# Last input-projection block contracted from the top, attention loads and biases started inside it

## The chip, the cores and the metric

The kernel runs on one core of a Trainium2 chip. The metric is the device time of one execution, in microseconds; lower is better. Engines: PE is TensorE, DVE VectorE, ACT ScalarE, POOL GpSimd, SP SyncE (which here only issues DMAs).

## The reference, cut to what matters

One encoder layer on x of 1024 positions by 2048 channels, float32:

```
h = rmsnorm(x); proj = h @ w_in            # 2048 x 6160: attention q,k,v; mLSTM q,k,v,o; gates
na = neighbourhood attention, 8 heads of 128, 16 x 64 grid, 8 x 16 window, relative bias, softmax
ml = mLSTM forward + backward, 4 heads, q,k through a width-5 convolution and silu first
x += concat(rmsnorm(na), ml) @ w_out
x += expert-choice FFN(rmsnorm(x))         # 16 experts, 128 tokens each, 1024 wide
out = rmsnorm(x)
```

Products are done in three parts: each float32 operand is split in a high and a low part, and high x high, high x low and low x high are summed.

## The kernel before, in words

**Stages.** In order: input projection (12 blocks of 512 output columns), attention, mLSTM, output projection, routing, experts, final norm. TensorE works through them in one fixed order; every engine has its own hand-written instruction order, and semaphores tie them.

**Projection block.** The normed input, transposed, stands in `a_hi` and `a_lo`, each 16 slices (contraction index k) of 4096 bytes a partition. The weights of a block come as 8 chunks of two slices through a ring of four (`raw`, filled by SP; `whi` by ACT, L902; `wlo` by DVE, L1226). Blocks 0 to 5 give `rows` (values, gates of the output), blocks 6 to 11 `feats` (mLSTM q,k; then attention q and k of heads 0 to 3 in blocks 8, 9, of heads 4 to 7 in 10, 11). `feats_block` (L1726 on, products at L1740) goes k = 0 to 15, for each k over four groups of two PSUM banks, 24 products of 128 x 512 per k. After each second k but the last it adds 1 to `w_used`, seven a block; in the last k each bank adds 1 to `bank_ready`. Blocks 6 to 11 run in a hardware loop on TensorE.

**Eviction and store.** DVE (`evict_feats`) multiplies each of 8 banks by the row scale into one of four `stage` slots; POOL (`store`) issues a DMA of it to memory and, when an earlier one has landed, frees its slot (`stage_free`). So banks 4 to 7 wait for landings of banks 0 to 3.

**Memory reuse.** Attention's buffers lie over the projection's. In bytes of a partition: `naq`, `nak`, `nav` (q, k, v of two heads) at 126464 to 159232, which is `a_hi` slices 8 to 15; `prob` from 192000 and `skew` (bias windows) from 200192, which is `a_lo` slices 8 and up; `qrows` at 175616, `a_lo` slices 4 and 5; `nmask`, `bias0`, `bias1` at 27648 to 55296, over the end of `raw`, over `whi` and the start of `wlo`; `na_out` at 60416, over the end of `wlo`, over `stage` and further.

**Start of the attention.** SP waits at L500 and L501 for block 11's `bank_ready`, then issues for heads 0 and 1: 8 windows `skew` (L432), q (L456), k (L457), 16 pieces of v (L466); then `qrows`, `decbc`, `mixg`; then heads 2 to 7, windows after `bias_ready`, q and k after `qk_done`, v after `pv_done` of the head two before. From head 4 on mLSTM loads stand between. POOL, after its stores of block 11, makes `nmask` (L752) and the bias tiles of head h (L757), six each.

**Attention itself.** 64 units, 8 a head. Unit v on TensorE: transpose of `prob` (L1790), score product of unit v + 3 (L1782), value product of unit v - 1 (L1802). DVE adds the bias and takes the maximum (L1382, L1386), ACT takes exp (L1004) and evicts the transpose (L1012), DVE writes the output `na_out` (L1395, `finish`). In unit 1 DVE waits for all stores of the projection, since `na_out` lies over `stage`. Outputs of units 0 and 1 lie over `wlo` only, the third is the first over `stage`.

Of the kernel before, what the change touches and what calls it, by code (L numbers as in the profile page):

```python
# [16 lines left out]
P = 128  # L17
SEQ, D = 1024, 2048
TT = SEQ // P
KD = D // P  # L20
NAH, HD = 8, 128
# [9 lines left out]
BW = 512  # L31
BLK = 12
ROWBLK = 6
OBLK = 4
CPB = KD // 2
RING = 4
GWC = KD * 16 + 32
QR, QC, WR, WC = 8, 16, 12, 32
# [50 lines left out]
def trunk(nc, t):  # L89
    ctx = ExitStack()  # L90
    with ctx:
# [9 lines left out]
        colm = sb("colm", [P, 3, WC])  # L101
        rowm = sb("rowm", [P, 2, WR])
# [13 lines left out]
        stage = sb("stage", [P, 4, BW], F32, proj)  # L116
# [3 lines left out]
        rstd_bc = sb("rstd_bc", [P, 1024], F32, proj)  # L120
        t3 = stage[:, 0:2, :].rearrange("p a b -> p (a b)")
        wide = ExitStack()
        a_hi = sb("a_hi", [P, KD, SEQ], F32R, wide)
# [23 lines left out]
        def place(at, *items):  # L147

            stack = ExitStack()
            if at > ROOM:  # L150
                stack.enter_context(nc.sbuf_tensor("below_" + items[0][0], [P, (at - ROOM) // 4], F32))
            made = [stack.enter_context(nc.sbuf_tensor(name, shape, F32)) for name, shape in items]
            stack.close()
            return made
# [6 lines left out]
        skew, = place(200192, ("skew", [P, 2, 16, 48]))  # L161
        nmask, bias0, bias1 = place(27648, ("nmask", [P, 6, WR, WC]), ("bias0", [P, 6, WR, WC]), ("bias1", [P, 6, WR, WC]))
        biases = (bias0, bias1)
        qrows, = place(175616, ("qrows", [P, 2, SEQ]))

        mv0, mv1, mbc0, kn1, wexp, kw, qkw = place(
            93696, ("mv0", [P, TT, DV + 1]), ("mv1", [P, TT, DV + 1]), ("mbc0", [P, 2, SEQ]), ("kn1", [P, TT, DK]),
# [60 lines left out]
        last = ExitStack()  # L228
        eraw = sb("eraw", [P, 2 * EDEEP, 1024], F32, last)
        last.close()  # L230
        last = ExitStack()
# [7 lines left out]
        ps = ctx.enter_context(nc.psum_tensor("ps", [P, 8, BW], F32))  # L239

        S = {}
# [15 lines left out]
        stsem = [S[f"st{i}"] for i in range(4)]  # L257
# [9 lines left out]
        nqsem, nkvsem, nbsem, mlsem = ([S[n + "0"], S[n + "1"]] for n in ("nq", "nkv", "nb", "ml"))  # L267
# [139 lines left out]
        def _(sp):  # L407
# [51 lines left out]
            def fetch_v(h):  # L459

                hb = h % 2
                for c in range(4):
                    for r in range(4):
                        at = bass.AP(t["rows"].tensor, (r * GW + KCOL[c]) * 3072 + h * HD,
                                     [[3072, WC], [4 * GW * 3072, 4], [1, HD]])
                        sp.dma_start(nav[r * WC:(r + 1) * WC, hb, c, :, :], at).then_inc(nkvsem[hb], 16)  # L466
# [29 lines left out]
                sp.dma_start(mo[h % 2][:, :, :], row_tiles(2048 + h * DV, 2048 + (h + 1) * DV)).then_inc(mosem[h % 2], 16)  # L496

            sp.wait_ge(S["rep_out"], 16 * QC)
            sp.wait_ge(S["bank_ready"], 8 * BLK)
            for m in stsem:  # L500
                sp.wait_ge(m, 32 * (BLK - 2))  # L501
            fetch_skew(0)
# [2 lines left out]
            fetch_skew(1)  # L505
            fetch_qk(1)
            fetch_v(1)
            sp.dma_start(qrows[:, :, :], t["q_rows"].rearrange("a p c -> p a c")).then_inc(S["gates_in"], 16)
            sp.dma_start(decbc[:, :, :, :].rearrange("p d h n -> p (d h n)"),
                         t["decays"].rearrange("a n -> (a n)").partition_broadcast(P)).then_inc(S["gates_in"], 16)  # L510
# [99 lines left out]
        def _(pool):  # L610
# [38 lines left out]
                pool.memset(s[:, :], 0.0).then_inc(S["gpad_zero"], 1)  # L649
            pool.memset(m_next[:, :], 0.0).then_inc(S["gpad_zero"], 1)  # L650

            def store(b, dst, last=False):

                for n in range(8):
                    past(S["bank_staged"], 8 * b + (n + 1))
                    pool.dma_start(dst(b, n), stage[:, n % 4, :]).then_inc(stsem[n % 4], 16)
                    for o in (n - 2,) if n < 7 else () if last else (5, 6, 7):
                        if o >= 0:
                            past(stsem[o % 4], 32 * b + 16 * (o // 4 + 1))
                            pool.sem_inc(S["stage_free"], 1)  # L660
# [74 lines left out]
                conv_block(b)  # L735
                store(b, to_feats)
            conv_block(BLK - 1)
            store(BLK - 1, to_feats, last=True)


            pool.wait_ge(S["bank_ready"], 8 * BLK)
            for hb in range(2):
                pool.memset(mv[hb][:, :, DV:DV + 1], 1.0).then_inc(S["ones_done"], 1)
            pool.wait_ge(S["colm_in"], 16 * (QR - 1))
            for h in range(NAH):
                pool.wait_ge(nbsem[h % 2], 128 * (h // 2 + 1))
                if h >= 2:
                    pool.wait_ge(S["scored"], 8 * (h - 1))
                for y in range(6):
                    half_, c = y // 3, y % 3  # L750
                    if h == 0:
                        pool.tensor_tensor(nmask[:, y, :, :], colm[:, c, :].unsqueeze(1).broadcast_to([P, WR, WC]),  # L752
                                           rowm[:, half_, :].unsqueeze(2).broadcast_to([P, WR, WC]), ALU.add)\
                            .then_inc(S["nmask_done"], 1)
                        pool.wait_ge(S["nmask_done"], y + 1)
                    r0, c0 = 4 - 4 * half_, 16 - 8 * c
                    pool.tensor_tensor(biases[h % 2][:, y, :, :], skew[:, h % 2, r0:r0 + WR, c0:c0 + WC], nmask[:, y, :, :], ALU.add)\  # L757
                        .then_inc(S["bias_ready"], 1)


            def weigh_keys(U):

# [54 lines left out]
            for U in range(MLU):  # L817
                h, u = U // 16, U % 16
# [21 lines left out]
            for i in range(OHB):  # L840
                b = i % OBLK
# [378 lines left out]
        def _(dve):  # L1220
# [100 lines left out]
            def evict_feats(b):  # L1321

                for n in range(8):
                    dve.wait_ge(S["bank_ready"], 8 * b + (n + 1))
                    dve.wait_ge(S["stage_free"], 8 * b + (n - 3))
                    c = slice((n % 2) * BW, (n % 2 + 1) * BW)
                    if b in (ROWBLK + 2, ROWBLK + 4):
                        tiles = "p (r w c) -> p r w c"
                        dve.tensor_tensor(stage[:, n % 4, :].rearrange("p (w r c) -> p r w c", w=4, c=QC),
                                          ps[:, n, :].rearrange(tiles, w=4, c=QC), rstd_bc[:, c].rearrange(tiles, w=4, c=QC),  # L1330
                                          ALU.mult).then_inc(S["bank_staged"], 1)
                    else:
                        dve.tensor_tensor(stage[:, n % 4, :], ps[:, n, :], rstd_bc[:, c], ALU.mult).then_inc(S["bank_staged"], 1)

            dve.wait_ge(S["rstd_bc_in"], 16)
            dve.wait_ge(S["gate_act"], 5)
# [72 lines left out]
            for v in range(NAU):  # L1409
                if v + NAD < NAU:  # L1410
                    score(v + NAD)
                if v == 1:
                    dve.wait_ge(S["conv_out"], 16 * 8)
                    for m in stsem:
                        dve.wait_ge(m, 32 * BLK)
                if v:
                    finish(v - 1)
                if v in GATEAT:
                    gate_columns(GATEAT.index(v))
                if v == 40:  # L1420
                    dve.wait_ge(S["cols_out"], 8)
                    dve.tensor_copy(thr[:, :, :, 0], cols[:, :, 3, 0, :].rearrange("p n h -> p h n")).then_inc(S["thr_done"], 1)
                    dve.tensor_copy(thr[:, :, ::-1, 1], cols[:, :, 3, 1, :].rearrange("p n h -> p h n")).then_inc(S["thr_done"], 1)
# [88 lines left out]
            for U in range(MLU):  # L1512
                h, u = U // 16, U % 16
# [63 lines left out]
            for q in range(ORING, OHB * KD):  # L1577
                out_low(q)
                i, k = q // KD - 1, q % KD - ORING + 1
# [82 lines left out]
            for p in range(ERING, NP):  # L1662
                kind, e, k = PAIRS[p - ERING]
# [39 lines left out]
        def _(pe):  # L1703
# [19 lines left out]
                    if k % 2 == 1 and k < KD - 1:  # L1723
                        last.then_inc(S["w_used"], 1)

            def feats_block(b, bank_wait=True):  # L1726

                for k in range(KD):
                    m = k // 2
                    if k % 2 == 0:  # L1730
                        pe.wait_ge(S["w_lo"], CPB * b + (m + 1))
                    for g in range(4):
                        at = (k % 2) * BW + g * P
                        hi, lo = whi[:, m % RING, at:at + P], wlo[:, m % RING, at:at + P]
                        for w, src in ((hi, a_hi), (hi, a_lo), (lo, a_hi)):
                            for h in range(2):
                                n = 2 * g + h
                                if k == 0 and w is hi and src is a_hi and bank_wait:
                                    pe.wait_ge(S["bank_staged"], 8 * b + (n - 7))
                                last = pe.matmul(ps[:, n, :], w, src[:, k, h * BW:(h + 1) * BW],  # L1740
                                                 start=(k == 0 and w is hi and src is a_hi),
                                                 stop=(k == KD - 1 and w is lo))
                                if k == KD - 1 and w is lo:
                                    last.then_inc(S["bank_ready"], 1)
                    if k % 2 == 1 and k < KD - 1:
                        last.then_inc(S["w_used"], 1)
# [15 lines left out]
                                         stop=(k == KD - 1 and a is a_lo))  # L1762
            last.then_inc(S["gates_ready"], 1)
            pe.wait_ge(S["gates_copied"], 1)
            with pe.Fori(ROWBLK, BLK) as b:
                feats_block(b)


            pe.wait_ge(S["ident_done"], 1)
# [147 lines left out]
            for U in range(MLU):  # L1917
                h, u = U // 16, U % 16
# [26 lines left out]
            for i in range(OHB):  # L1945
                for k in range(KD):
# [8 lines left out]
                    hi, lo = ohi[:, k % ORING, :], olo[:, k % ORING, :]  # L1955
# [156 lines left out]
```

## Time and profile before

| | us |
|---|---|
| median of 3 runs | 2973.02 (2972.45 to 2973.21) |
| profiled execution | 2972.88 |
| its span | 2971.3 |
| projection block 11 ends on TensorE | 1082.85 after the span's start |
| first score product | 1095.85 |
| first mLSTM product | 1218.27 |

Times inside the profile count from the span's start. "Idle before" an instruction is put down to what released it. The granted clock is TensorE's: 1.00 is 2.4 GHz, 0.5 is 1.2 GHz, values between are a mix over the stretch.

### The profile page before, as it was taken

The numbers are of one execution on the slowest core, as the hardware profiler recorded it, in microseconds if no ns is written. First come the engines' busy times: TensorE is split into PE (matmuls) and PEld (weight loads), VectorE is DVE, ScalarE is ACT, GpSimd is POOL, SyncE is SP. The second block draws the span as 40 slices with busy tenths as digits, with TensorE's granted clock in tenths as the row PEclk, the third lists the DMA queues.
The fourth block names the chain that finished last, engine by engine and source line by source line (L and its number), as shares of the span: only waits on it lengthen the run. The fifth ranks groups of instructions, "written<-read, shape, count | busy, mean of one in ns | idle before, by whom it ended". The sixth has DMA issues, their size and how long they took to land.

```text
span 2971.3 us, 33520 instructions
## 1 busy us (share of the span) xinstructions
PE 2781.7 (94%) x12738; PEld 2281.5 (77%) x12738; DVE 1583.1 (53%) x1679; ACT 1324.5 (45%) x1458; POOL 374.5 (13%) x593
## 2 busy tenths in 40 slices
PE   8999999999999989989999944999999999999992
PEld 7888888888888867768777733888888888888881
DVE  4110111311233326674332358888888888888883
ACT  5111111201111115654232323777777777777773
POOL 1200000020011023571010101010000000000000
PEclk9999999999999999999999977999999999999996
DMA  8322212122222238534354455999999999999987
GB/s 308 93 76 78 76 51 78 57 98 78 78 104 101 78 117 245 179 103 139 131 167 135 162 177 197 381 396 405 401 388 406 401 405 404 403 403 403 402 319 269
DMA packets 193516, 660.53 MB, mean 222 GB/s; under 512 B 24025, under 2 KB 49128, under 8 KB 170608
## 3 DMA queue, kind: packets, MB, share of 16 engines
q1 hardware_dynamic: 169088, 564.52, 50.2%
q0 software_dynamic: 24304, 94.39, 9.7%
q8 instruction: 74, 1.21, 0.2%
q14 instruction: 50, 0.41, 0.0%
HBM read 585.99 MB, written 72.79 MB: 222 GB/s over the span
## 4 chain that ended last, share of the span: by engine, by line
PE 87%; issue 4%; DVE 3%; POOL 3%; DMA 1%; SPq 1%; ACT 0%; POOLq 0%; DVEq 0%; ACTq 0%
PE ps L2024 23%; PE ps L1740 17%; PE ps L1718 6%; PE ps L1720 6%; PE ps L1719 6%; PE ps L1961 4%; PE ps L1963 4%; PE ps L1962 4%; PE ps L2047 4%; PE ps L2045 4%; PE ps L2046 4%; PE ps L2003 1%; PE ps L1942 1%; PE ps L1782 1%; PE ps L1761 1%
## 5 line engine op out<-in xcount | busy, mean ns | idle before, releaser
L1635 DVE TENSOR_TENSOR elo<-eraw,ehi 128x2048 fp32r<-128x2048 f32 x384 | 874.4, 2292 | 137.1 <-ACT ehi L1146 130.6
L1146 ACT ACTIVATE ehi<-eraw 128x2048 fp32r<-128x2048 f32 x384 | 733.2, 1919 | 246.8 <-PE ps L2024 163.8
L1226 DVE TENSOR_TENSOR wlo<-raw,whi 128x1024 fp32r<-128x1024 f32 x96 | 117.6, 1225 | 704.9 <-ACT whi L902 704.8
L902 ACT ACTIVATE whi<-raw 128x1024 fp32r<-128x1024 f32 x96 | 101.7, 1059 | 732.6 <-PE ps L1740 393.5
L2024 PE MATMUL ps<-ehi,xh 128*128 128x512 f32 x960 | 373.5, 389 | 0.0
L2024 PE MATMUL ps<-elo,xh 128*128 128x512 f32 x960 | 373.4, 389 | 0.0
L1718 PE MATMUL ps<-whi,a_hi 128*128 128x512 f32 x768 | 299.9, 390 | 11.3 <-DVE a_lo L1236 11.3
L1719 PE MATMUL ps<-wlo,a_hi 128*128 128x512 f32 x768 | 299.6, 390 | 0.0
L1720 PE MATMUL ps<-whi,a_lo 128*128 128x512 f32 x768 | 299.5, 390 | 0.0
L2024 PE MATMUL ps<-ehi,xl 128*128 128x512 f32 x960 | 256.6, 389 | 0.0
L1740 PE MATMUL ps<-a_hi,whi 128*128 128x512 f32 x768 | 236.8, 389 | 1.8 <-DVE t L1258 1.6
L1740 PE MATMUL ps<-a_lo,whi 128*128 128x512 f32 x768 | 236.5, 389 | 0.0
L1740 PE MATMUL ps<-a_hi,wlo 128*128 128x512 f32 x768 | 236.4, 389 | 0.0
L1509 DVE TENSOR_TENSOR olo<-oraw,ohi 128x512 fp32r<-128x512 f32 x128 | 88.5, 697 | 249.9 <-ACT ohi L1073 249.8
L2024 PEld LDWEIGHTS ps<-ehi,xl 128*128 128x128 f32 x960 | 180.2, 188 | 37.4
L2024 PEld LDWEIGHTS ps<-elo,xh 128*128 128x128 f32 x960 | 180.2, 188 | 37.4
L2024 PEld LDWEIGHTS ps<-ehi,xh 128*128 128x128 f32 x960 | 180.2, 188 | 37.4
L1961 PE MATMUL ps<-ohi,a_hi 128*128 128x512 f32 x512 | 204.9, 400 | 3.6 <-DVE mh L1469 3.6
L2045 PE MATMUL ps<-ehi,hh 128*128 128x512 f32 x512 | 202.9, 396 | 0.0
L1963 PE MATMUL ps<-ohi,a_lo 128*128 128x512 f32 x512 | 200.7, 392 | 0.0
L1962 PE MATMUL ps<-olo,a_hi 128*128 128x512 f32 x512 | 200.5, 392 | 0.0
L2047 PE MATMUL ps<-ehi,hl 128*128 128x512 f32 x512 | 199.5, 390 | 0.0
(246 smaller groups left out, 3892.3 us busy)
## 6 DMA issues: line engine op xcount, KB each, us to landing
eraw<-in_w_gate SPq DMA_DIRECT2D x256, 512.0 KB
eraw<-in_w_up SPq DMA_DIRECT2D x256, 512.0 KB
eraw<-in_w_down SPq DMA_DIRECT2D x128, 1024.0 KB
raw<-in_w_stream SPq DMA_DIRECT2D x96, 512.0 KB
oraw<-in_w_stream SPq DMA_DIRECT2D x128, 256.0 KB
scr_rows<-stage POOLq DMA_DIRECT2D x48, 256.0 KB, 2.3
scr_feats<-stage POOLq DMA_DIRECT2D x48, 256.0 KB, 2.3
t<-in_xT SPq DMA_DIRECT2D x16, 512.0 KB, 5.6
```

The costliest lines, as they stand in the source:

```text
L1146: act.activation(ehi[:, p % ERING, :], flat2(eraw[:, 2 * (p % EDEEP):2 * (p % EDEEP) + 2, :]), ACT.Copy)\
L1635: dve.tensor_tensor(elo[:, p % ERING, :], flat2(eraw[:, 2 * (p % EDEEP):2 * (p % EDEEP) + 2, :]), ehi[:, p % ERING, :].bitcast(F32), ALU.s ...
L1718: pe.matmul(ps[:, n, :], xs, hi, start=(k == 0), stop=False)
L1719: pe.matmul(ps[:, n, :], xs, lo, start=False, stop=False)
L1720: last = pe.matmul(ps[:, n, :], src_lo[:, k, n * P:(n + 1) * P], hi, start=False, stop=(k == KD - 1))
L1740: last = pe.matmul(ps[:, n, :], w, src[:, k, h * BW:(h + 1) * BW], start=(k == 0 and w is hi and src is a_hi), stop=(k == KD - 1 and w is lo))
L1961: pe.matmul(bank, xs, hi, start=(k == 0), stop=False)
L1962: pe.matmul(bank, xs, lo, start=False, stop=False)
L1963: last = pe.matmul(bank, a_lo[:, KORD[k], n * P:(n + 1) * P], hi, start=False, stop=(k == KD - 1))
L2024: last = pe.matmul(gu_bank(e, c), a[:, k, :], w[:, p % ERING, c * BW:(c + 1) * BW], start=(k == 0 and a is hi and w is ehi), stop=(k == KD ...
L2045: pe.matmul(y_bank(e, c), hh[:, h, :], ehi[:, p % ERING, at], start=(k == 0), stop=False)
L2047: last = pe.matmul(y_bank(e, c), hl[:, h, :], ehi[:, p % ERING, at], start=False, stop=(k == KE - 1))
```

## The change

Block 11 is taken out of TensorE's loop and contracts the slices 15 down to 0 (`back=True`); the host lays its weights in that order. SP waits for four of block 11's chunks to be used instead of all its banks before the loads of heads 0 and 1, and for all banks only before `qrows`. POOL makes all six masks after the fifth chunk and head 0's bias tiles after the fifth, sixth and seventh, ahead of block 11's stores. Banks 4 to 7 of block 11 go to four spare slots, `stage_end`, over the first half of `raw`, so their evictions wait for no store. POOL waits once, after the fourth store, for all four to land. DVE's wait for all stores moves from unit 1 to unit 3.

```diff
+        stage_end, = place(19456, ("stage_end", [P, 4, BW]))
@@ sync
-            sp.wait_ge(S["bank_ready"], 8 * BLK)
+            sp.wait_ge(S["w_used"], 7 * (BLK - 1) + 4)
...
             fetch_v(1)
+            sp.wait_ge(S["bank_ready"], 8 * BLK)
             sp.dma_start(qrows[:, :, :], t["q_rows"].rearrange("a p c -> p a c")).then_inc(S["gates_in"], 16)
@@ gpsimd
             conv_block(BLK - 1)
-            store(BLK - 1, to_feats, last=True)
...
+            pool.wait_ge(S["colm_in"], 16 * (QR - 1))
+            pool.wait_ge(S["w_lo"], CPB * BLK)
+            pool.wait_ge(S["w_used"], 7 * (BLK - 1) + 5)
+            for y in range(6):
+                mask_tile(y)
+            pool.wait_ge(nbsem[0], 128)
+            pool.wait_ge(S["nmask_done"], 6)
+            for y in range(6):
+                if y in (2, 4):
+                    pool.wait_ge(S["w_used"], 7 * (BLK - 1) + 5 + y // 2)
+                bias_tile(0, y)
+            for n in range(8):
+                pool.wait_ge(S["bank_staged"], 8 * (BLK - 1) + n + 1)
+                src = stage if n < 4 else stage_end
+                pool.dma_start(to_feats(BLK - 1, n), src[:, n % 4, :]).then_inc(stsem[n % 4], 16)
+                if n == 3:
+                    for m in range(4):
+                        pool.wait_ge(stsem[m], 32 * (BLK - 1) + 16)
 
             pool.wait_ge(S["bank_ready"], 8 * BLK)
...
-            for h in range(NAH):
+            for h in range(1, NAH):
...
@@ vector
-                    dve.wait_ge(S["stage_free"], 8 * b + (n - 3))
+                    if b < BLK - 1 or n < 4:
+                        dve.wait_ge(S["stage_free"], 8 * b + (n - 3))
+                    to = stage if b < BLK - 1 or n < 4 else stage_end
...
-                if v == 1:
+                if v == 3:
                     dve.wait_ge(S["conv_out"], 16 * 8)
                     for m in stsem:
                         dve.wait_ge(m, 32 * BLK)
@@ tensor
-            def feats_block(b, bank_wait=True):
+            def feats_block(b, back=False):
...
-                    m = k // 2
+                    m, kk = k // 2, KD - 1 - k if back else k
...
-                                last = pe.matmul(ps[:, n, :], w, src[:, k, h * BW:(h + 1) * BW],
+                                last = pe.matmul(ps[:, n, :], w, src[:, kk, h * BW:(h + 1) * BW],
...
-            with pe.Fori(ROWBLK, BLK) as b:
+            with pe.Fori(ROWBLK, BLK - 1) as b:
                 feats_block(b)
+            feats_block(BLK - 1, back=True)
@@ host
+    w_mix = np.concatenate([w_mix[:BLK - 1], w_mix[BLK - 1:, ::-1]], axis=0).reshape(BLK, CPB, 2, P, BW).transpose(0, 1, 3, 2, 4)
```

## Rows read from the trace of the kernel before

**Rows 1.** The page, chain that ended last, shares by engine.

```profile
PE 87%; issue 4%; DVE 3%; POOL 3%; DMA 1%; SPq 1%; ACT 0%; POOLq 0%; DVEq 0%; ACTq 0%
```

**Rows 2.** The chain in order of time, around 1087: start, us, what.

```profile
1087.02 8.69 DMA nak<-scr_feats
```

**Rows 3.** Timeline of PE: start, us, engine, line, op, count, [idle before, releaser].

```profile
1095.85 4.18 PE L1782 MATMUL ps<-nak,naq 128*128 128x384 f32 x6 [13.00 <-DMA nak<-scr_feats]
...
1103.19 0.49 PE L1790 MATMUL ps<-ident,prob 128*128 128x128 f32 x3
...
1104.16 0.83 PE L1802 MATMUL ps<-nav,probT 128*128 128x128 f32 x6
1104.83 0.49 PE L1790 MATMUL ps<-ident,prob 128*128 128x128 f32 x3
```

**Rows 4.** Windows: stretch, length, busy time of each engine, clock, DMA share, GB/s.

```profile
1087.00:1096.00 9.00, 0.15 (x1) 0.18 (x2) 0.00 (x0) 0.00 (x0) 7.04 (x11) 0.54 0.93 276
1096.00:1110.00 14.00, 14.00 (x69) 10.23 (x70) 8.13 (x35) 7.81 (x22) 10.22 (x11) 0.81 0.73 207
```

**Rows 5.** Timeline of SP's queue from 1082: issue start, us of issuing.

```profile
1082.92 3.59 SPq L432 DMA_DIRECT2D skew<-scr_rpb_rep  x8
...
1087.56 9.66 SPq L466 DMA_DIRECT2D nav<-scr_rows  x16
...
1101.91 7.55 SPq L466 DMA_DIRECT2D nav<-scr_rows  x16
```

**Rows 6.** Timeline of ACT in block 11.

```profile
1028.55 1.06 ACT L902 ACTIVATE whi<-raw 128x1024 fp32r<-128x1024 f32 x1 [8.78 <-PE ps L1740]
1039.42 1.06 ACT L902 ACTIVATE whi<-raw 128x1024 fp32r<-128x1024 f32 x1 [9.82 <-PE ps L1740]
```

**Rows 7.** Timeline of POOL after block 11.

```profile
1087.91 0.54 POOL L656 DMA_DIRECT2D scr_feats<-stage  x1 [1.21 <-DMA scr_feats<-stage]
...
1089.34 0.83 POOL L752 TENSOR_TENSOR nmask<-colm,rowm 128x384 f32<-128x384 f32 x1 [0.73 <-DMA skew<-scr_rpb_rep]
...
1102.64 5.82 POOL L757 TENSOR_TENSOR bias<-skew,nmask 128x384 f32<-128x384 f32 x6 [2.08 <-DMA skew<-scr_rpb_rep]
```

**Rows 8.** Timeline of DVE at the seam.

```profile
1078.58 2.65 DVE L1333 TENSOR_TENSOR stage<-ps,rstd_bc 128x512 f32<-128x512 f32 x4 [36.84 <-PE ps L1740]
...
1085.62 0.69 DVE L1333 TENSOR_TENSOR stage<-ps,rstd_bc 128x512 f32<-128x512 f32 x1 [0.93 <-POOLq L660]
1097.63 0.56 DVE L1382 CUSTOM_DVE_ANT_0 prob<-ps,bias 128x384 f32<-128x384 f32 x1 [11.32 <-PE ps L1782]
```

**Rows 9.** Timeline of ACT, first exp of the attention.

```profile
1098.42 0.61 ACT L1004 ACTIVATE prob<-prob,ntop 128x384 f32<-128x384 f32 x1 [55.59 <-DVE ntop L1386]
```

**Rows 10.** Timeline of TensorE's weight loads, first transpose.

```profile
1099.18 0.23 PEld L1790 LDWEIGHTS ps<-ident,prob 128*128 128x128 f32 x1 [0.30 <-ACT prob L1004]
```

**Rows 11.** Block 11's eight stores, from the rows of their tile, 1075 to 1100.

```profile
DMA to landing us min/median/max: 2.3/3.0/8.5
```

**Rows 12.** Waits of SP's queue, 1105 to 1200: us, times, longest.

```profile
SPq L466 <- PE ps L1802: 2.1, 3, 0.9
```

**Rows 13.** Timeline of PE, first score products of heads 5 and 6.

```profile
1165.00 0.91 PE L1782 MATMUL ps<-nak,naq 128*128 128x384 f32 x2 [2.09 <-DMA nak<-scr_feats]
...
1182.81 1.24 PE L1782 MATMUL ps<-nak,naq 128*128 128x384 f32 x2 [2.74 <-DMA nak<-scr_feats]
```

**Rows 14.** Timeline of PE in the mLSTM stage.

```profile
1323.45 0.63 PE L1900 MATMUL ps<-ident,mh 128*128 128x128 f32 x4 [1.88 <-DVE a_lo L1489]
```

**Rows 15.** Windows around that idle time and after 1165.

```profile
1320.00:1328.00 8.00, 6.10 (x31) 4.78 (x29) 7.34 (x19) 3.80 (x13) 6.33 (x11) 1.00 0.36 132
1165.00:1169.00 4.00, 4.00 (x16) 3.13 (x17) 1.26 (x6) 1.16 (x3) 3.12 (x4) 0.65 0.83 241
```

**Rows 16.** DMA queues in the expert stage, 1990 to 2080: packets, MB, share.

```profile
q8 instruction: 3, 0.05, 0.2%
```

**Rows 17.** Window of the expert stage.

```profile
2000.00:2020.00 20.00, 20.00 (x93) 16.68 (x92) 17.09 (x12) 16.55 (x14) 5.31 (x3) 1.00 1.03 402
```

More of the change, by code:

```diff
@@ L650, in _, with store @@
             pool.memset(m_next[:, :], 0.0).then_inc(S["gpad_zero"], 1)
-            def store(b, dst, last=False):
+            def store(b, dst):
                 for n in range(8):
@@ L656, in store @@
                     pool.dma_start(dst(b, n), stage[:, n % 4, :]).then_inc(stsem[n % 4], 16)
-                    for o in (n - 2,) if n < 7 else () if last else (5, 6, 7):
+                    for o in (n - 2,) if n < 7 else (5, 6, 7):
                         if o >= 0:
@@ L737, in _, with mask_tile, bias_tile @@
             conv_block(BLK - 1)
-            store(BLK - 1, to_feats, last=True)
+            def mask_tile(y):
+                half_, c = y // 3, y % 3
+                pool.tensor_tensor(nmask[:, y, :, :], colm[:, c, :].unsqueeze(1).broadcast_to([P, WR, WC]),
+                                   rowm[:, half_, :].unsqueeze(2).broadcast_to([P, WR, WC]), ALU.add).then_inc(S["nmask_done"], 1)
+            def bias_tile(h, y):
+                half_, c = y // 3, y % 3
+                r0, c0 = 4 - 4 * half_, 16 - 8 * c
+                pool.tensor_tensor(biases[h % 2][:, y, :, :], skew[:, h % 2, r0:r0 + WR, c0:c0 + WC], nmask[:, y, :, :], ALU.add)\
+                    .then_inc(S["bias_ready"], 1)
+            pool.wait_ge(S["colm_in"], 16 * (QR - 1))
[16 more added lines that the diff above has]
+                        pool.wait_ge(stsem[m], 32 * (BLK - 1) + 16)
             pool.wait_ge(S["bank_ready"], 8 * BLK)
@@ L743, in _ @@
                 pool.memset(mv[hb][:, :, DV:DV + 1], 1.0).then_inc(S["ones_done"], 1)
-            pool.wait_ge(S["colm_in"], 16 * (QR - 1))
-            for h in range(NAH):
+            for h in range(1, NAH):
                 pool.wait_ge(nbsem[h % 2], 128 * (h // 2 + 1))
@@ L749, in _ @@
                 for y in range(6):
[L750 to L758, printed above, removed]
+                    bias_tile(h, y)
             def weigh_keys(U):
@@ L1332, in evict_feats @@
                     else:
-                        dve.tensor_tensor(stage[:, n % 4, :], ps[:, n, :], rstd_bc[:, c], ALU.mult).then_inc(S["bank_staged"], 1)
+                        dve.tensor_tensor(to[:, n % 4, :], ps[:, n, :], rstd_bc[:, c], ALU.mult).then_inc(S["bank_staged"], 1)
             dve.wait_ge(S["rstd_bc_in"], 16)
@@ L1737, in feats_block @@
                                 n = 2 * g + h
-                                if k == 0 and w is hi and src is a_hi and bank_wait:
+                                if k == 0 and w is hi and src is a_hi:
                                     pe.wait_ge(S["bank_staged"], 8 * b + (n - 7))
-                                last = pe.matmul(ps[:, n, :], w, src[:, k, h * BW:(h + 1) * BW],
+                                last = pe.matmul(ps[:, n, :], w, src[:, kk, h * BW:(h + 1) * BW],
                                                  start=(k == 0 and w is hi and src is a_hi),
@@ L2087 @@
     cols_ = [w[:, 2048:3072], w[:, 4096:6144], w[:, 3072:4096], w[:, 0:512], w[:, 1024:1536], w[:, 512:1024], w[:, 1536:2048]]
-    w_mix = np.concatenate(cols_, axis=1).reshape(CPB, 2, P, BLK, BW).transpose(3, 0, 2, 1, 4)
+    w_mix = np.concatenate(cols_, axis=1).reshape(KD, P, BLK, BW).transpose(2, 0, 1, 3)
+    w_mix = np.concatenate([w_mix[:BLK - 1], w_mix[BLK - 1:, ::-1]], axis=0).reshape(BLK, CPB, 2, P, BW).transpose(0, 1, 3, 2, 4)
     w_o = w_out[0].reshape(CPB, 2, P, OBLK, BW).transpose(3, 0, 2, 1, 4)
```

## The prediction

> **What bounds the kernel now.** I read the chain's shares first: TensorE holds 87% of the span [rows 1], so the change can only win where TensorE stands still. Then the chain in order of time around the last projection block (block 11) and the first scores: one piece there is no work at all, 8.69 us from the issue of head 0's keys to their landing [rows 2]. TensorE's timeline gives the whole hole: the first score product starts at 1095.85 after 13.00 us idle, released by `nak` [rows 3], so the last projection product ended at 1082.85. By stages, the granted clock is 0.54 of full in 1087 to 1096 and 0.81 in 1096 to 1110 [rows 4], that is, TensorE fell from 2.4 to 1.2 GHz while it idled and ran its first products at 1.2. SP's own rows say why the keys were late: its first attention load is issued at 1082.92, when block 11 is done; eight bias windows and head 0's q come before `nak`, and heads 0 and 1 together take SP until 1109.46 [rows 5].
>
> **The change part by part.**
> *When SP is released.* The new condition is four of eight weight chunks of block 11 used. A chunk takes 10.87 us (ScalarE refills its ring once per chunk, 1028.55 to 1039.42 [rows 6]); TensorE ends at 1082.85, so the fourth chunk ends near 1082.85 - 4 x 10.87 = 1039.4. By then, contracting from slice 15 down, slices 15 to 8 are used up, and `naq`, `nak`, `nav`, `prob`, `skew` lie in slices 8 and up. SP's 52 DMAs for heads 0 and 1 took it from 1082.92 to 1109.46, 26.5 us [rows 5]; now 1039.4 to 1065.9, and with 8.7 us to land [rows 2] all is there at 1075, some 8 us before TensorE wants it. SP was idle in that time, and its weight loads are all issued. SP then waits for the whole block again before `qrows`, `decbc`, `mixg`: issued near 1083 instead of 1109.5, needed in the thirteenth unit, so free. SP's next load, bias windows of head 2, needs only the bias tiles of head 0.
> *POOL.* Masks start with the fifth chunk (1050.2): six at 0.83 [rows 7], done near 1056; biases of head 0 at 5.82/6 = 0.97 each [rows 7], the last pair after the seventh chunk (1072.0), done near 1074. DVE stages its first bank at 1079.27 (1078.58 + 0.69 [rows 8]), so the stores behind these waits lose nothing; cover 5 us, one for one beyond it. Head 1's biases, before at 1102.64 [rows 7], run 1087.2 to 1093; DVE wants the first at 1094.
> *Evictions.* Four bank evictions take 2.65 us, 0.66 each [rows 8]; the last now ends at 1086.3 (1085.62 + 0.69), because slots come back through POOL. A product takes 10.87/48 = 0.226 us and banks finish in pairs every six products, the last pair at 1082.62 and 1082.85; with spare slots DVE ends at about 1082.65 + 2 x 0.66 = 1084.0. Before, the nak wait covered all of this; now it is on the path.
> *What is late next.* TensorE does three score products at once (1082.85 to 1084.8), then waits for the first transposable probabilities: DVE score at 1084.0; 0.79 us from score to exp (1097.63 [rows 8], 1098.42 [rows 9]); 0.76 from exp to TensorE's load of them (1099.18 [rows 10]); about 0.15 for that load (0.23 at the low clock): first transpose at 1085.75, TensorE idle 1 us. Then two times transpose plus score product, 0.97 each (1103.19 to 1104.16), and one value product, 0.67 (to 1104.83 [rows 3]): third transpose at 1088.36. ScalarE's three exps (0.61 [rows 9]) and one eviction end just in time for the value product. Before, the third transpose started at 1103.19. Difference 14.8 us: 13.0 of wait, 1.8 because the fill runs at full clock and partly under evictions. Bounds of the fill, qk to third transpose: not over the 7.34 us of before, not under TensorE's own 4.6 us of products; so the gain is between 13.0 and 15.8. I take 14.8, since each step of it has a row.
> *Stores and the moved DVE wait.* Stores 4 to 7 now wait once for the first four to land, then issue within 2.2 us, near 1084.8 to 1086.9, instead of up to 1088.4 [rows 7]. DVE waits for all landings before its third output instead of its first: the earlier one would stand near 1088.6, the new one stands after score 6, near 1091.8. Landing took 2.3 to 8.5 us [rows 11], the long ones beside head 0's q and k loads. Now `qrows` (1 MB) and head 2's windows are beside them, so 1089 to 1095.4. TensorE asks for that output two units (3.3 us) later, and three scores are queued ahead, so a landing up to about 1093.7 costs nothing and the worst 1.7 us. I take nothing.
> The Trainium skill (SBUF — State Buffer, "SBUF: two separate sides") says that a DMA issued by GpSimd has its descriptors written by GpSimd and stands still while a two-port VectorE operation holds the shared port. By it these stores, now issued beside DVE's scores, could each lose up to one DVE operation, 0.56 us; the cover of 1.9 us takes that, and the sum stays.
> *Unrolled block 11.* 384 products leave TensorE's loop and become straight code. The expert stage is straight code of like density: TensorE's queue fetches three pieces of 16 KB in 90 us [rows 16], so block 11 (87 us) means about three more; and there, at a DMA share of 1.03, TensorE is busy 20.00 of 20.00 us [rows 17]. So 0; the loads of heads 0 and 1 beside it write other slices at a lower share. Reordered weights cost the device nothing.
> *After the start.* In the attention SP is held by TensorE's value products already (2.1 us in three waits [rows 12]), at 1.64 us a unit; SP's loads of head 2 on move with TensorE, 0.2 us ahead at best. The waits for keys of heads 5 and 6, idle 2.09 and 2.74 us [rows 13], each followed by slow products (clock 0.65 over 4 us, 1.4 us lost [rows 15]), cost some 7.6 us in all; they come from mLSTM loads put between, so they move along and stay. Nothing downstream has an absolute time, so 14.8 reaches the end.
>
> **Sum.** Profiled execution 2972.88 (span 2971.3 and 1.6 around it), minus 14.8, is 2958.1; the median of the runs is 0.14 higher: 2958.2 us. Its own range is 2956.7 to 2959.7.
>
> **Rivals.**
> A, *the clock falls in the fill.* TensorE goes from dense products to 1 us idle and gaps. For: idles of 2.09 and 2.74 us [rows 13] were followed by products at half rate. Against: an idle of 1.88 us [rows 14] left the clock at 1.00 [rows 15]. Price: one spell as after 1165, 1.4 us [rows 15]: 2959.6. With late stores (above) beside it: up to 2961.3.
> The Trainium skill (TensorE: Matmul & The Clock Gate, "A second HAM failure mode: psum-queue depth-cycling") says that many short idles between groups of products are enough to make the clock swing. The first three units have such gaps; by it A is what happens, yet the mLSTM stage at 1320 to 1328 [rows 15] has them all along and kept 1.00.
> B, *given back later.* The queue behind heads 2 and up is disturbed: their loads wait for TensorE while `qrows`, stores and windows crowd 1083 to 1092, and the key waits of heads 5 and 6 double. For: SP has little spare time in the attention. Against: three 13 us head cycles lie between. Price 7.6: 2965.8.
> C, *more.* SP comes early enough that those key waits vanish: 2950.6. Against: `nav` of head 4 cannot be issued before head 3's neighbour slot is read, so SP's lead is gone at head 4. A part of it, 2 us, is easier: 2956.
> D, *slower.* In the second half of block 11 TensorE fetches fresh code beside SP's 26 us of loads (DMA share up to 0.93 [rows 4]). If each of three pieces stalled it, it would decide from 14.8/3 = 4.9 us a piece; at 6 us a piece, 18 - 14.8 = 3.2 lost: 2976.2. For: the loop's body before was fetched once. Against: rows 16 and 17.
> E, *the change doesn't do what it says*, a late bias or load keeps TensorE waiting as before: the margins above (8 us for loads, 10 for head 0's first biases) speak against; gain then under 5.9: 2969.
>
> **How the numbers follow.** Forecast 0.72, A 0.12, C (mostly its part) 0.06, B 0.03, E 0.04, D 0.03. 0.2% is 5.9 us: faster is forecast, A, C and most of B, 0.92; within it 0.05 (E and a worse B); slower 0.03. The range takes the forecast, C's part and A with late stores: 2955.7 to 2962.
>
> **What would show it.** Right: SP's first windows issued near 1039.4; TensorE's idle at the seam about 1 us, released by an exp; first score product near 1083, third transpose near 1088.4; clock 1.00 through 1080 to 1110; no DVE wait on stores after score 6 beyond 2 us; key waits of heads 5 and 6 of 2 to 3 us, 15 us earlier. Wrong: any TensorE idle in block 11, a 0.5 clock spell before 1100, or key waits that grew.

## The result

The changed kernel takes 2955.25 us (median of five, 2953.33 to 2958.23) against 2973.02 before; ratio 0.9944, 95% interval 0.9931 to 0.9956. Both kernels were timed twice more, which gave 0.9947 (0.9934 to 0.9961) and 0.9951 (0.9937 to 0.9964), with medians of 2955.81 against 2972.1 and 2957.8 against 2971.82. So the gain is 14 to 18 us, 16 as a mean of the three; forecast were 14.8 us and 2958.2. The first median lies 0.45 us below the stated range of 2955.7 to 2962, the other two lie inside it.

The profiled executions differ by 2972.88 - 2955.25 = 17.6 us. Times below are those of the span. The seam is the stretch from the end of block 11 to the third transpose. In the changed kernel block 11 ends at 1081.71 on TensorE, 1.13 us earlier than before.

TensorE's timeline of the changed kernel, answering to [rows 3]:

```profile
1081.09 0.62 PE L1764 MATMUL ps<-a_hi,wlo 128*128 128x512 f32 x2
1081.55 2.10 PE L1807 MATMUL ps<-nak,naq 128*128 128x384 f32 x6
1084.26 0.55 PE L1815 MATMUL ps<-ident,prob 128*128 128x128 f32 x3 [0.62 <-ACT prob L1026]
...
1086.94 0.49 PE L1815 MATMUL ps<-ident,prob 128*128 128x128 f32 x3
```

The score products follow the last projection product with no gap at all; the 13.00 us idle has become 0.62, released by an exp. From block end to the third transpose it is 5.23 us (1081.71 to 1086.94) instead of 20.35 (1082.84 to 1103.19).

DVE at the seam, answering to [rows 8], and ACT's first exp, to [rows 9]:

```profile
1077.44 2.65 DVE L1357 TENSOR_TENSOR stage<-ps,rstd_bc 128x512 f32<-128x512 f32 x4 [36.84 <-PE ps L1764]
1080.16 2.65 DVE L1357 TENSOR_TENSOR stage_end<-ps,rstd_bc 128x512 f32<-128x512 f32 x4
1082.72 0.55 DVE L1406 CUSTOM_DVE_ANT_0 prob<-ps,bias 128x384 f32<-128x384 f32 x1
```

```profile
1083.50 0.61 ACT L1026 ACTIVATE prob<-prob,ntop 128x384 f32<-128x384 f32 x1 [41.81 <-DVE ntop L1410]
```

Eight evictions run without a break and the first score starts on their heels. SP's queue, answering to [rows 5]:

```profile
1038.26 3.58 SPq L433 DMA_DIRECT2D skew<-scr_rpb_rep  x8
...
1056.99 7.55 SPq L467 DMA_DIRECT2D nav<-scr_rows  x16
1081.74 0.39 SPq L510 DMA_DIRECT2D qrows<-scr_q_rows  x1
...
1083.27 4.34 SPq L433 DMA_DIRECT2D skew<-scr_rpb_rep  x8
1091.39 0.35 SPq L457 DMA_DIRECT2D naq<-scr_feats  x1
...
1098.63 7.46 SPq L467 DMA_DIRECT2D nav<-scr_rows  x16
```

The loads of heads 0 and 1 are issued from 43.45 us before block 11's end, the last of them 17 us before it. In this stretch SP stands idle three times: before `qrows`, before head 2's q (3.8 us) and before head 2's v (6.4 us). POOL, answering to [rows 7]:

```profile
1049.25 4.79 POOL L744 TENSOR_TENSOR nmask<-colm,rowm 128x384 f32<-128x384 f32 x6 [7.71 <-PE ps L1764]
1054.18 2.00 POOL L751 TENSOR_TENSOR bias<-skew,nmask 128x384 f32<-128x384 f32 x2
...
1070.91 2.00 POOL L751 TENSOR_TENSOR bias<-skew,nmask 128x384 f32<-128x384 f32 x2 [8.89 <-PE ps L1764]
...
1083.74 2.14 POOL L768 DMA_DIRECT2D scr_feats<-stage_end  x4 [2.82 <-DMA scr_feats<-stage]
```

Masks and biases of head 0 are done 9 us before the block's end. The windows (columns as in [rows 4]) show TensorE busy all the time beside the loads, and a clock that no longer falls. From its only idle time (0.16 us, near its start) to its end, block 11 takes 83.03 us, to 0.01, in the profile of every kernel here:

```profile
1038.00:1066.00 28.00, 28.00 (x125) 23.18 (x124) 1.23 (x1) 3.38 (x3) 9.32 (x11) 1.00 0.71 197
```

```profile
1087.00:1096.00 9.00, 9.00 (x61) 7.54 (x60) 6.42 (x30) 6.21 (x18) 8.46 (x9) 1.00 0.73 270
1096.00:1110.00 14.00, 14.00 (x96) 11.76 (x95) 9.33 (x43) 9.09 (x27) 2.14 (x3) 1.00 0.41 98
```

Block 11's stores (to [rows 11]) and DVE's wait for them, which now stands in unit 3:

```profile
DMA to landing us min/median/max: 2.3/3.8/5.6
```

```profile
DVE pinv L1416 <- DMA scr_feats<-stage_end: 0.6, 1, 0.6
```

And the key waits of heads 5 and 6, answering to [rows 13]:

```profile
1147.14 0.91 PE L1807 MATMUL ps<-nak,naq 128*128 128x384 f32 x2 [0.48 <-DMA nak<-scr_feats]
1164.74 1.43 PE L1807 MATMUL ps<-nak,naq 128*128 128x384 f32 x2 [4.20 <-DMA nak<-scr_feats]
```

Where the 17.6 us come from, by the start times of transposes (unit 2, unit 34, unit 63) and of the first output projection product (1334.93 before, 1317.36 now):

| stretch | before | changed | gained |
|---|---|---|---|
| start to end of block 11 | 1082.84 | 1081.71 | 1.1 |
| end of block 11 to transpose 2 | 20.35 | 5.23 | 15.1 |
| transpose 2 to 34 | 53.87 | 53.87 | 0.0 |
| transpose 34 to 63 | 58.57 | 56.89 | 1.7 |
| transpose 63 to output projection | 119.30 | 119.66 | -0.4 |
| from there to the end | 1636.4 | 1636.4 | 0.0 |

The second row is the change. Whether the first and fourth are, the experiments had to tell.

### The profile page after: what moved, and what is told of

It reads as the page before. It is cut to its first block, busy times and chain, and to the rows that moved or that the text cites. A ratio compares the mean times of both kernels' runs of the same rounds, so it can differ in the third digit from the quotient of the medians.

```text
span 2953.7 us, 33485 instructions
## 1 busy us (share of the span) xinstructions
PE 2776.9 (94%) x12738; PEld 2278.7 (77%) x12738; DVE 1582.5 (54%) x1679; ACT 1324.4 (45%) x1458; POOL 375.8 (13%) x593
## 4 chain that ended last, share of the span: by engine, by line
PE 89%; issue 4%; DVE 3%; POOL 2%; DMA 1%; ACT 0%; POOLq 0%; SPq 0%; DVEq 0%; ACTq 0%
PE ps L2049 24%; PE ps L1764 17%; PE ps L1742 6%; PE ps L1743 6%; PE ps L1744 6%; PE ps L1986 4%; PE ps L1988 4%; PE ps L1987 4%; PE ps L2072 4%; PE ps L2071 4%; PE ps L2070 4%; PE ps L1827 1%; PE ps L1807 1%; PE ps L2028 1%; PE ps L1967 1%
```

## The experiments

The table has the same stretches for every kernel run; the seam is the second row of the table above, "first half" transposes 2 to 34, "second half" 34 to 63.

| kernel | median us | seam | first half | second half |
|---|---|---|---|---|
| before | 2973.02 | 20.35 | 53.87 | 58.57 |
| changed | 2955.25 | 5.23 | 53.87 | 56.89 |
| r1 changed again | 2955.81 | 5.23 | 53.87 | 56.24 |
| r2 before again | 2972.57 (one run) | 19.17 | 53.87 | 59.41 |
| r3 block only | 2970.89 | 21.19 | 53.87 | 58.31 |
| r4 windows early | 2967.44 | 12.69 | 56.83 | 57.00 |
| r5 bias late | 2963.42 | 12.19 | 53.87 | 56.62 |
| r6 shared slots | 2964.78 | 13.63 | 53.87 | 58.20 |
| r7 wait in unit 1 | 2958.84 | 5.22 | 58.03 | 55.69 |
| r8 mLSTM loads early | 2953.50 | 5.22 | 59.39 | 49.77 |
| r9 mLSTM loads in block | 2948.33 | 5.23 | 53.87 | 50.05 |
| r10 shared slots, quiet SP | 2959.54 | 9.11 | 53.86 | 56.35 |
| r11 changed, third time | 2957.80 | 5.22 | 53.87 | 58.65 |

The times of r1 to r4 share runs of the kernel before with a median of 2972.1, r5 to r8 2971.54, r9 to r11 2971.82. Medians of one kernel differ by up to 2.6 us between these groups, so differences of 2 us are read in the trace only.

**r1, r2 and r11: both kernels again, for their scatter.**

> The changed kernel once more, unaltered. What is to be told apart: of the 17.6 us between the two profiled executions, 1.2 us lie before the first projection product (idle 11.3 against 10.1 us) and about 1.8 us in the key waits of attention heads 5 and 6. Theory (both are scatter between executions): the first product's idle and the two key waits come out differently again, by 1 us or more, and the seam after block 11 (end of the block to third transpose, 5.2 us) is the same within 0.1. Rival (the change shortens the key waits): the wait of head 5 is again near 0.5 us and that of head 6 near 4.2, and the sum of both is below that of before. Time 2954 to 2958 either way.

> The kernel before once more, unaltered, for its scatter. Theory: first idle 10 to 11.5 us, key waits of heads 5 and 6 somewhere between 0.5 and 4.5 us each, seam again 13.0 us of idle within 0.2. Rival (key waits belong to the kernel): 2.1 and 2.7 us again within 0.3.

> The changed kernel unaltered, on the chip of this comparison, as its reference and as a third look at its key waits. Both theories: 2954 to 2957. If the sum of the second half of the attention belongs to the kernel it is again 56 to 57 us (before: 58.3 to 59.4); if it is scatter it may come out above 58.

The key waits, TensorE's timeline of r2 and of r11:

```profile
1161.63 0.91 PE L1782 MATMUL ps<-nak,naq 128*128 128x384 f32 x2 [0.67 <-DMA nak<-scr_feats]
...
1180.69 1.65 PE L1782 MATMUL ps<-nak,naq 128*128 128x384 f32 x2 [5.65 <-DMA nak<-scr_feats]
```

```profile
1147.59 0.91 PE L1807 MATMUL ps<-nak,naq 128*128 128x384 f32 x2 [1.25 <-DMA nak<-scr_feats]
1165.21 1.65 PE L1807 MATMUL ps<-nak,naq 128*128 128x384 f32 x2 [4.21 <-DMA nak<-scr_feats]
```

The kernel before waits 2.09 and 2.74 us once and 0.67 and 5.65 the other time: what one head saves, the next one waits. The second half took 58.57, 59.41 and 58.31 in the kernels with before's loads, and 56.89, 56.24 and 58.65 in the changed one. After two profiles that seemed to belong to the change; the third lies inside the other group. The variants r5, r6, r7 and r10 load heads 0 and 1 where the changed kernel does: the mean of all seven such profiles is 56.9 against 58.8 for the three others. That leans to a gain of some 1.8 us there, but two of the seven reach 58.2 and more, and no run shows a cause. So the fourth row of the table is not shown to be the change's. The idle before the first projection product was 11.29 and 10.13 us in the kernel before, 10.11, 10.39 and 10.22 in the changed one, 9.6 to 10.0 in the variants: 1.2 of the 17.6 us is that. The seam of the changed kernel is 5.22 to 5.23 in every profile; that of before is 19.2 to 20.4, and 21.2 in r3 with the same loads, since there the landing of a load is on the path.

**r3: the unrolled, reversed block alone.** With it go the reversed slices and the host's order of the weights, as in the change; all else as before:

```diff
-            with pe.Fori(ROWBLK, BLK) as b:
+            with pe.Fori(ROWBLK, BLK - 1) as b:
                 feats_block(b)
+            feats_block(BLK - 1, back=True)
```

> The kernel before with block 11 unrolled and contracted from slice 15 down, weights laid out for it, and nothing else moved: loads, masks, biases, evictions as before. Theory (the unrolled block costs nothing, its code is fetched ahead): same time as before within 1 us, seam idle 13.0 us, three more code pieces. Rival (a code fetch stalls TensorE): each of three pieces costs some, the block gets longer than 87.0 us.

Ratio to before 0.9997 (0.9987 to 1.0006), idle at the seam 14.62 us (13.00 and 12.57 in the kernel before), block 11 the same 83.03 us. Its list of DMA queues for 990 to 1085 has the fetched code, which that of the kernel before has not:

```profile
q8 instruction: 3, 0.05, 0.2%
```

Three pieces, as estimated, and no time that shows. Unrolling and reversing are free here and alone worth nothing.

**r4: only head 0's windows early.**

```diff
             fetch_skew(0)
+            sp.wait_ge(S["bank_ready"], 8 * BLK)
             fetch_qk(0)
             fetch_v(0)
...
-            sp.wait_ge(S["bank_ready"], 8 * BLK)
```

> The changed kernel, but of head 0 and 1 only head 0's bias windows are loaded inside block 11; q, k, v of head 0 and everything of head 1 wait for the whole block again. Theory (the seam is the path of q and k: issue, queue behind other traffic, landing): nak is issued near block end + 0.6 us and lands 4 to 7 us later, so TensorE idles 5 to 8 us instead of 13.0 and the clock falls in it; time 5 to 9 us above the changed kernel (2960 to 2965). Rival (what counted before was the bias chain on POOL, which stays early here): idle under 2 us, time within 2 us of the changed kernel.

```profile
1086.45 3.71 PE L1807 MATMUL ps<-nak,naq 128*128 128x384 f32 x6 [5.24 <-DMA nak<-scr_feats]
1093.13 0.94 PE L1827 MATMUL ps<-nav,probT 128*128 128x128 f32 x6 [0.89 <-DMA nav<-scr_rows]
1100.93 0.91 PE L1807 MATMUL ps<-nak,naq 128*128 128x384 f32 x2 [1.61 <-DMA nak<-scr_feats]
```

Idle 5.24 as the theory said, so q and k are the path; the seam grows by 7.5 us, in which 0.89 is a wait for head 0's v. The median is 11.6 above r1, more than the 5 to 9 expected: with SP late, the keys of head 1 (1.61) and head 2 (0.74 at 1115.51) come late too (first half 56.83).

**r5: masks and biases after the stores.** POOL's two steps in their old place, loads and slots as in the changed kernel.

```diff
             conv_block(BLK - 1)
...
-            pool.wait_ge(S["w_used"], 7 * (BLK - 1) + 5)
-            for y in range(6):
-                mask_tile(y)
...
-                bias_tile(0, y)
             for n in range(8):
                 pool.wait_ge(S["bank_staged"], 8 * (BLK - 1) + n + 1)
...
             pool.wait_ge(S["bank_ready"], 8 * BLK)
...
+            for y in range(6):
+                mask_tile(y)
+                pool.wait_ge(S["nmask_done"], y + 1)
+                bias_tile(0, y)
             for h in range(1, NAH):
```

> The changed kernel, but POOL makes masks and head 0's bias tiles after block 11's stores, as before; loads stay inside block 11, spare slots stay. Theory (the second wait of the seam is POOL's bias): stores end near block end + 4.2, mask and first bias take 1.9 more, so DVE's first score starts some 6.2 us after the block's end instead of 1.0; TensorE idles 5 to 6 us after its three score products and the clock falls: 5 to 8 us above the changed kernel. Rival (POOL's masks and biases were hidden behind DVE's pace anyway): within 1 us of it.

```profile
1088.86 0.90 PE L1810 MATMUL ps<-ident,prob 128*128 128x128 f32 x3 [5.82 <-ACT prob L1021]
```

Seam 12.19, 7.0 us longer, 7.6 us in the median against r1: as expected. The early loads and the spare slots without the biases keep about half the gain.

**r6 and r10: shared slots, with and without SP's loads beside them.**

```diff
                 for n in range(8):
-                    if b < BLK - 1 or n < 4:
-                        dve.wait_ge(S["stage_free"], 8 * b + (n - 3))
-                    to = stage if b < BLK - 1 or n < 4 else stage_end
+                    dve.wait_ge(S["stage_free"], 8 * b + (n - 3))
+                    to = stage
```

POOL stores and frees slots as before. r10 has, beside this, in SP:

```diff
             sp.wait_ge(S["bank_ready"], 8 * BLK)
+            for m in stsem:
+                sp.wait_ge(m, 32 * BLK)
             sp.dma_start(qrows[:, :, :], t["q_rows"].rearrange("a p c -> p a c")).then_inc(S["gates_in"], 16)
```

> The changed kernel, but banks 4 to 7 of block 11 go to the four old slots and wait for the landing of earlier stores, as before. Theory: the last eviction ends at block end + 3.5 us instead of + 1.0 (before: 1086.3 against 1082.85), or later since qrows is beside it, and the first score starts as much later: 2.5 to 4 us slower than the changed kernel. Rival (the depth of the pipeline takes it): within 0.5 us.

> The kernel with shared slots for banks 4 to 7 (9 us slower than the changed one), but SP issues qrows and what follows only when all stores of block 11 have landed. Theory (there the fifth store took 7.2 us to land because 1.4 MB of SP's loads was beside it, and the last eviction waited for it): landings 2.3 to 3 us, last eviction at block end + 3.5, idle before the first transpose 3 us instead of 7.7; 3 to 6 us faster than with shared slots alone: 2959 to 2961. Rival (slots come back slowly by themselves): no gain within 1 us.

DVE in r6, then in r10; below each the landing of block 11's eight stores:

```profile
1083.29 0.69 DVE L1355 TENSOR_TENSOR stage<-ps,rstd_bc 128x512 f32<-128x512 f32 x1 [0.16 <-POOLq L770]
1089.59 0.69 DVE L1355 TENSOR_TENSOR stage<-ps,rstd_bc 128x512 f32<-128x512 f32 x1 [5.61 <-POOLq L770]
```

```profile
DMA to landing us min/median/max: 2.3/2.6/7.2
```

```profile
1082.88 0.69 DVE L1357 TENSOR_TENSOR stage<-ps,rstd_bc 128x512 f32<-128x512 f32 x1 [0.17 <-POOLq L772]
1084.30 0.69 DVE L1357 TENSOR_TENSOR stage<-ps,rstd_bc 128x512 f32<-128x512 f32 x1 [0.72 <-POOLq L772]
```

```profile
DMA to landing us min/median/max: 2.3/2.3/2.6
```

The expectation for r6 (2.5 to 4 us) was wrong by far: the seam grows by 8.4 us and the median by 9.0 against r1. I had taken the slots' return as it was before; but now `qrows` and the windows are issued at block end. Beside them the fourth store (not the fifth, as r10's expectation has it), whose slot the eighth eviction needs, took 7.2 us, and the next two 6.9. With SP quiet all land within 2.6 us, and the seam shrinks from 13.63 to 9.11, as the theory said; TensorE idles 7.71 us before the first transpose in r6, 2.83 in r10 and 0.62 in the changed kernel. The median of r10, 2959.54, is inside its forecast. Shared slots cost 8.4 us of seam in this schedule, and 3.9 where SP's loads wait for the stores. Of these 3.9, 2.2 are idle time and 1.4 the clock, which is 0.64 over 1086 to 1090.

**r7: DVE's wait in unit 1.**

```diff
-                if v == 3:
+                if v == 1:
```

> The changed kernel, but DVE's wait for all stores stands in unit 1 again, not in unit 3. Theory (stores 4 to 7 land 4 to 8 us after block end, DVE comes to unit 1 near block end + 5.4): DVE waits 1 to 4 us; the scores queued ahead take 1.9 of it, so 0 to 2 us slower. Rival (no store is late): no wait, same time, and this part of the change is idle.

```profile
DVE pinv L1416 <- DMA scr_feats<-stage_end: 4.0, 1, 4.0
```

```profile
1091.62 0.91 PE L1827 MATMUL ps<-nav,probT 128*128 128x128 f32 x6 [2.25 <-DVE na_out L1419]
...
1092.69 1.28 PE L1807 MATMUL ps<-nak,naq 128*128 128x384 f32 x2
1093.76 1.49 PE L1827 MATMUL ps<-nav,probT 128*128 128x128 f32 x6
```

DVE waits 4.0 us, and the first half grows by 4.16. TensorE idles only 2.25 of the 4.0: the products queued ahead take the other 1.7, near the 1.9 expected. What the expectation left out is the clock. It is 0.61 over 1092 to 1096 and 0.96 over the next 4 us, which is 1.7 us lost; two score products take 1.28 us there, and 0.81 at full clock (1088.91 in the changed kernel). Two units later the same stores cost 0.6 us of DVE's time and none of TensorE's. The move of one line is worth 4 us in the trace (1 to 3 us in the medians, against r11 and r1).

**r8 and r9: the mLSTM loads, moved into the time SP now has.** r8:

```diff
                 fetch_qk(h)
+                if h == 2:
+                    fetch_ml_qk(0)
+                    fetch_ml_v(0)
+                    fetch_ml_m(0)
+                    fetch_ml_s(0)
+                elif h == 3:
+                    fetch_ml_v(1)
+                    fetch_ml_m(1)
                 sp.wait_ge(S["pv_done"], 8 * (h - 1))
                 fetch_v(h)
-                if h == 4:
...
```

> The changed kernel, but the loads of the first two mLSTM heads (6 MB) move from between attention heads 4 to 7 to heads 2 and 3, into the time in which SP now waits for TensorE (3.8 and 6.4 us). Theory (the key waits of heads 5 and 6 come from these loads standing before the keys in SP's queue): both key waits vanish, 5 to 7 us faster than the changed kernel, 2949 to 2951; risk: the v of head 2 lands late behind them, up to 2 us back. Rival (the queue is simply full in that stage): waits appear elsewhere, at heads 2, 3 or 7, and the time is the same within 1.5 us.

```profile
1112.75 0.94 PE L1826 MATMUL ps<-nav,probT 128*128 128x128 f32 x6 [0.67 <-DMA nav<-scr_rows]
1129.34 1.65 PE L1826 MATMUL ps<-nav,probT 128*128 128x128 f32 x6 [2.75 <-DMA nav<-scr_rows]
```

Both held in part: the key waits are gone (second half 49.77), and 5.5 us come back in the first half, with waits for v of heads 2 and 3 (0.67 and 2.75 us idle). The median, 2953.50, is 1.8 to 4.3 us under the three of the changed kernel, not the 5 to 7 expected. r9 places most of these bytes where the queues were empty:

```diff
             fetch_v(1)
+            sp.wait_ge(S["conv_out"], 16 * 8)
+            sp.wait_ge(S["w_used"], 7 * (BLK - 1) + 5)
+            fetch_ml_qk(0)
+            sp.wait_ge(S["w_used"], 7 * (BLK - 1) + 6)
+            fetch_ml_m(0)
+            sp.wait_ge(S["w_used"], 7 * (BLK - 1) + 7)
+            fetch_ml_s(0)
+            fetch_ml_v(1)
             sp.wait_ge(S["bank_ready"], 8 * BLK)
...
                 fetch_qk(h)
+                if h == 2:
+                    fetch_ml_v(0)
+                    fetch_ml_m(1)
                 sp.wait_ge(S["pv_done"], 8 * (h - 1))
                 fetch_v(h)
```

> The changed kernel, but 4 of the 6 MB of loads for the first two mLSTM heads go into the second half of block 11, each behind the chunk that frees its place (q and k after the fifth, the m rows of head 0 after the sixth, its scale rows and the v of head 1 after the seventh); the v of head 0 and the m rows of head 1 follow the keys of attention head 2. Theory (the earlier try gained 7 us in heads 5 and 6 and gave 5.5 back because 6 MB stood before the v of heads 2 and 3): no key wait at heads 5 and 6, second half of the attention near 50 us instead of 56.2 to 56.9, first half 54 to 55, so 5 to 7 us under the changed kernel: 2948 to 2951. Rival (these loads now delay qrows, the windows of head 2 or block 11's stores at the seam): the seam or DVE's wait in unit 3 grows by 1 to 4 us and half of it is lost.

Windows of the second part of the attention, the changed kernel and r9:

```profile
1140.00:1199.00 59.00, 54.26 (x360) 45.37 (x360) 33.27 (x150) 34.97 (x96) 23.61 (x25) 0.97 0.91 260
```

```profile
1140.00:1193.00 53.00, 52.92 (x366) 44.71 (x365) 35.14 (x153) 35.24 (x96) 23.66 (x25) 1.00 0.65 193
```

No wait in either half; seam and first half untouched. 2948.33 us (2948.09 to 2949.5), 9.5 below the changed kernel beside it, ratio to before 0.9919 (0.9905 to 0.9933). Of the 9.5, 6.2 to 8.6 is the second half; the rest is within what the other stretches vary by. It is the fastest kernel of this study. Both runs move the place of the mLSTM loads in SP's queue and the bytes that travel beside the keys (DMA share 0.91 and 0.65 in the windows above); which of the two makes the keys late they do not tell apart.

## Why the prediction was right

- *SP's release*: put at block end - 43.45, measured 1081.71 - 1038.26 = 43.45. Loads done long before they are wanted: right.
- *POOL*: masks at block end - 32.5, last bias at - 8.8; both within 0.2 us of the forecast. r5 gives the step's worth, 7.0 us. r3 and r4 show that no single part does it: the block alone brings nothing, and all parts but the early loads of q, k, v and head 1's windows bring 7.7 of the 15.1 (20.35 to 12.69).
- *Evictions*: last one at block end + 1.1, forecast + 1.15. Right, but the price of the shared slots was read from the old traffic, 2.3 us (1086.3 to 1084.0); r6 measured 8.4 with the new traffic. In the sum it made no difference, since the changed kernel never pays either.
- *Fill*: forecast 5.5 us from block end to third transpose, measured 5.23. TensorE idles 0.62 instead of 1.0. The first exp starts 1.79 us after block end (forecast 1.94), and the first transpose 0.76 after it; the sum had added 0.15 for a weight load to these 0.76. (Its steps add up to 1085.70 for the first transpose, where it has 1085.75.)
- *Clock*: 1.00 throughout; A did not happen. TensorE idled 0.62 before the first transpose and its clock held, as the trace of before had it after 1.88 us. The many short gaps, by which the Trainium skill (TensorE: Matmul & The Clock Gate, "A second HAM failure mode: psum-queue depth-cycling") has the clock swing, were not there either: besides the 0.62 the timeline of TensorE has no gap from block end to 1110. So the fill did not put that rule to the test.
- *Stores*: landings up to 5.6 us, inside the forecast 2.3 to 8.5. The wait in unit 3 cost DVE 0.6 us and TensorE nothing. The 1.9 us of cover is near what r7 shows in unit 1, 1.7. A wait beyond the cover was priced one for one; r7 adds 1.7 us of low clock to 2.25 of idle time. The loss of up to 0.56 us a store beside DVE's scores does not show in the issue of the four stores: 2.14 us for four, 0.54 each, as for one alone [rows 7]. Whether it is in their landing no run tells; nor did a row show those scores, which read PSUM, to be two-port operations.
- *Code*: three pieces, no time. D is out (r3).
- *After the start*: the first half moved along whole, 53.87 in each. The sign "key waits of heads 5 and 6 of 2 to 3 us" did not come: they are 0.48 and 4.20. Their sum is 4.68 against 4.83, and the forecast that they "move along and stay" holds for that sum within its scatter. That they come from the mLSTM loads is shown by r8 and r9. SP's lead at head 2 is 0.8 us, not 0.2: its v is issued 11.7 us after the third transpose (1098.63 - 1086.94), before it was 12.5 (1115.65 - 1103.19). C was the right mechanism with the wrong key: not an earlier SP, but other places for these loads free the 6 to 9 us (r9).
- *Size*: 14.8 forecast, 15.1 at the seam of the two profiles (13.9 against r2), 14 to 18 in the medians. That forecast and seam agree to 0.3 us is partly luck, since the seam of before alone varies by more. The 3 us between 2958.2 and 2955.25 are the fourth row and the start of the kernel, which vary from run to run.

## What to carry to other kernels

When a stage's buffers lie over the operands of the stage before, the order of the contraction decides when they come free: reverse it so that the wanted half is used up first, and move everything that the first product of the next stage needs (loads, masks, evictions), since each part left behind cost about half the gain at the seam here (7.5, 7.0 and 8.4 of 15.1 us in r4, r5 and r6). Price a wait on a slot by the traffic that the change puts beside it, not by the old one. Put a wait for stores a few units behind the start of a pipeline: in unit 3 it cost nothing here, in unit 1 4.2 us, nearly half of it the clock that fell in the idle time.

## What the runs showed of the hardware

A 256 KB store lands in 2.3 to 2.6 us with the queues quiet (r10) and takes up to 7.2 with 1.4 MB of loads issued within some 6 us beside it (r6); with the loads of heads 0 and 1 beside it, it was up to 8.5 (before) and 9.6 (r3). TensorE's products ran at their full pace (28.00 of 28.00 us busy, clock 1.00) beside loads at a DMA share of 0.71 into neighbouring slices of the same buffer. The length of an idle time did not alone decide TensorE's clock: after 2.25 us the granted clock was 0.61 over 1092 to 1096 (r7), after 2.53 us it was 1.00 over 1160 to 1168 (r4, before a key product at 1159.11). The idle before the kernel's first product differs by up to 1.7 us between executions (9.56 in r10, 11.29 in before), and the same loads, in the same order, left 2.09 and 2.74 us of waits in one execution and 0.67 and 5.65 in another.
